# Weights of the dense experts in parts of 80 and 48 first keys instead of two halves of 64, with both weighted one-hots in one instruction and the pair sums in fewer cells

## What is computed

```
def peer_ffn(h, w_q, sub_keys, u_tab, v_tab):
    q = (xc @ w_q).reshape(t, PEER_HEADS, 2, PEER_QDIM // 2)
    sc = jnp.einsum('thpc,hpnc->thpn', q, sub_keys)
    v_half, i_half = lax.top_k(sc, PEER_TOPK_HALF)
    cand = (v_half[:, :, 0, :, None] + v_half[:, :, 1, None, :]).reshape(t, PEER_HEADS, -1)
    cand_idx = (i_half[:, :, 0, :, None] * PEER_NKEYS + i_half[:, :, 1, None, :]).reshape(t, PEER_HEADS, -1)
    top_s, pos = lax.top_k(cand, PEER_TOPK)
    expert = jnp.take_along_axis(cand_idx, pos, axis=-1)
    g = jax.nn.softmax(top_s, axis=-1)
    act = jax.nn.gelu(jnp.einsum('thkd,td->thk', u_tab[expert], xc), approximate=False)
    return jnp.einsum('thk,thkd->td', g * act, v_tab[expert])
```

## Time and profile before

| | |
|---|---|
| median of the runs | 2077.0 us |
| the profiled execution | 2068.39 us, span 2066.6 us |
| TensorE busy | 2007.3 us (97%) |
| VectorE busy | 1622.2 us (78%) |
| ScalarE busy | 857.9 us (42%) |
| GpSimd busy | 385.0 us (19%) |
| moved by DMA | 511.17 MB, mean 247 GB/s |
| granted TensorE clock, mean | 0.992 of full speed |

### The profile page before, as it was taken

One profiled execution on the slowest core, in us unless ns is written; L12 is line 12 of the kernel. 1 busy time (PEld: TensorE's weight loads), 2 busy tenths in 40 slices (PEclk: granted clock), 3 DMA queues, 4 the chain that ended last, 5 costly groups with the idle time before them and its releaser, 6 DMA issues.

```text
span 2066.6 us, 35237 instructions
## 1 busy us (share of the span) xinstructions
PE 2007.3 (97%) x12408; PEld 1791.5 (87%) x12408; DVE 1622.2 (78%) x3208; ACT 857.9 (42%) x1653; POOL 385.0 (19%) x262
## 2 busy tenths in 40 slices
PE   8999999999999999999999999999999999999998
PEld 6888887779999999977887887899999998778786
DVE  6899886865799276699999967639964756999997
ACT  6557454545101100055565666531101002555665
POOL 0000000000024233303243100000352322232440
PEclk9999999999999999999999999999999999999999
DMA  6554344415389989867799853335998988678995
GB/s 258 198 203 163 114 139 156 138 67 174 133 337 341 368 321 327 300 241 229 262 351 356 294 184 117 113 117 195 391 353 309 346 306 317 224 243 281 371 377 181
DMA packets 132634, 511.17 MB, mean 247 GB/s; under 512 B 15004, under 2 KB 15132, under 8 KB 129856
## 3 DMA queue, kind: packets, MB, share of 16 engines
q1 hardware_dynamic: 95680, 375.81, 51.7%
q0 software_dynamic: 36864, 134.23, 17.6%
HBM read 508.94 MB, written 1.05 MB: 247 GB/s over the span
## 4 chain that ended last, share of the span: by engine, by line
PE 64%; DVE 16%; DMA 5%; issue 2%; ACT 2%; SPq 0%; DVEq 0%; ACTq 0%
PE bank L2383 30%; PE bank L344 8%; PE bank L346 8%; PE bank L345 8%; DVE tile_lo L2705 5%; DMA wbuf<-in_peer_v 3%; PE bank L2413 3%; PE bank L2414 3%; DVE x_tok L2258 2%; DMA wbuf<-in_peer_u 2%; PE bank L2282 1%; DVE w_parts L2708 1%; DVE e_hot_first L2274 1%; DVE e_hidden L2290 1%; DVE tile_lo L274 1%
## 5 line engine op out<-in xcount | busy, mean ns | idle before, releaser
L2383 PE MATMUL bank<-h_dense,wbuf 128*128 128x192 f32 x4096 | 679.7, 327 | 3.7 <-ACT e_stage L2467 2.4
L2383 PEld LDWEIGHTS bank<-h_dense,wbuf 128*128 128x128 f32 x4096 | 664.2, 190 | 6.0 <-issue 4.9
L2512 ACT ACTIVATE tile_hi<-wbuf 128x1024 fp32r<-128x1024 f32 x248 | 263.0, 1060 | 246.1 <-DMA wbuf<-in_peer_v 202.3
L2705 DVE TENSOR_TENSOR tile_lo<-wbuf,tile_hi 128x1024 fp32r<-128x1024 f32 x256 | 311.0, 1215 | 37.7 <-ACT tile_hi L2512 27.4
L2244 POOL DMA_INDIRECT e_gbuf<-in_peer_v,e_row_at x128 | 227.1, 1774 | 484.3 <-DVE x_tok L2258 445.8
L2494 ACT ACTIVATE e_hidden<-bank 128x384 f32<-128x384 f32 x128 | 62.7, 490 | 603.2 <-PE bank L2383 603.2
L2244 POOL DMA_INDIRECT e_gbuf<-in_peer_rows,e_row_at x128 | 155.8, 1218 | 470.1 <-DVE e_dots L2252 239.0
L2413 PE MATMUL bank<-tile_hi,w_parts 128*128 128x512 f32 x512 | 208.5, 407 | 11.1 <-DVE w_parts L2708 10.4
L274 DVE TENSOR_TENSOR tile_lo<-wbuf,tile_hi 128x1024 fp32r<-128x1024 f32 (+2 forms) x117 | 140.3, 1212 | 80.1 <-ACT tile_hi L266 79.2
L2414 PE MATMUL bank<-tile_lo,w_parts 128*128 128x512 f32 x512 | 200.4, 391 | 0.0
L344 PE MATMUL bank<-tile_hi,w_parts 128*128 128x512 f32 x512 | 200.1, 391 | 0.0
(11 more groups left out here) (391 smaller groups left out, 3500.3 us busy)
## 6 DMA issues: line engine op xcount, KB each, us to landing
wbuf<-in_peer_u SPq DMA_DIRECT2D x256, 512.0 KB, 5.7
wbuf<-in_peer_v SPq DMA_DIRECT2D x256, 512.0 KB, 5.0
wbuf<-in_w_in SPq DMA_DIRECT2D x16, 2048.0 KB, 7.7
wbuf<-in_peer_q SPq DMA_DIRECT2D x32, 512.0 KB, 3.8
wbuf<-in_hyb_in SPq DMA_DIRECT2D x16, 512.0 KB, 3.7
wbuf<-in_mla_uq SPq DMA_DIRECT2D x9, 512.0 KB, 3.4
wbuf<-in_mla_in SPq DMA_DIRECT2D x8, 528.0 KB, 4.2
wbuf<-in_w_v SPq DMA_DIRECT2D x2, 2048.0 KB, 7.3
```

Source lines behind the costliest of these rows:

```text
L2383: last = nc.tensor.matmul(bank[:, j // 2 % 2, j % 2 * S:j % 2 * S + DENSE], ring[:, slot, k * P:(k + 1) * P], h_dense[:, k, :], start=(k = ...
L2512: nc.scalar.activation(tile_hi[:, slot, 0:D], ring[:, slot, 0:D], ACT.Copy).then_inc(hi_done, 1)
L2705: nc.vector.tensor_tensor(tile_lo[:, slot, 0:D], ring[:, slot, 0:D], tile_hi[:, slot, 0:D].bitcast(F32), ALU.subtract).then_inc(lo_done, 1)
```

## The change

- `PARTS`: the first part is first keys 0 to 79 with groups of 6 tokens (32 groups, 12 matmuls of 80 columns each), the second is keys 80 to 127 with groups of 8 (24 groups, 16 matmuls of 48 columns). `HALF`, `GROUP` and `NGROUP` go.
- The picks are turned after key 79 of U, and the 32 groups of the first part come after keys 80 to 118: after four of every five keys. Keys 120 to 127 have none. The 24 groups of the second part come after every third key from 0 to 69 of V.
- The share's two parts lie together in `pick_parts`, and one multiplication makes both weighted one-hots, twice as many elements as each of the two had. A matmul reads every fourth element of them, before every second.
- `TAKEN` and `LAST_TAKE`: VectorE takes rows 36 to 85 during weighted U (before 36 to 77), rows 86 to 91 during the weighted keys of V (before 78 to 87), the rest by key 118 (before 116).
- The gelu of the dots and the product with the shares come in two pieces (48 and 16), after keys 93 and 103.
- The pair sums of a head are 17 rows of 8 (the first score of one half with all 16 of the other, then each further one with the first 8), 136 cells in place of 256; the place of a pick is turned back into its two indices by a few more small steps.
- `dense_turned` turns 128 x 128 for both halves of the tokens, where the first was 64 x 64; the second writes over what is too much.

```diff
-    HALF = NKEYS // 2
-    GROUP = 8
+    PARTS = ((0, 80, 6), (80, 48, 8))
+    FIRST_KEYS = PARTS[0][1]
     WEIGHT_ONE = 4096.0
-    NGROUP = DENSE // GROUP
+    NGROUPS = [DENSE // group for start, keys, group in PARTS]
...
+    pick_parts = picks_T[:, 2:4, :].rearrange("p w t -> p (w t)").rearrange("p (i w m) -> p i w m", w=2, m=2)
...
-    is_first = [sb(f"{tag}_is_first{b}", [P, PAIRS, HALF, 2], F16) for b in range(2)]
-    hot_first = [sb(f"{tag}_hot_first{b}", [P, 2, PAIRS, HALF, 2], F16) for b in range(2)]
-    hot_second = [sb(f"{tag}_hot_second{b}", [P, PAIRS, NKEYS, 2], F16) for b in range(2)]
+    is_first = [sb(f"{tag}_is_first{b}", [P, most_first], F16) for b in range(2)]
+    hot_first = [sb(f"{tag}_hot_first{b}", [P, 2 * most_first], F16) for b in range(2)]
+    hot_second = [sb(f"{tag}_hot_second{b}", [P, most_second], F16) for b in range(2)]
...
+        weighted_first = hot_first[b][:, 0:2 * group * keys].rearrange("p (i a w m) -> p i a w m", a=keys, w=2, m=2)
...
-        b = n % 2
-        tokens = bass.ds(GROUP * n, GROUP)
-        def pairs(j, keys):
...
-        nc.vector.tensor_tensor(is_first[b][:, :, :, :], wide[:, half * HALF:(half + 1) * HALF, :].unsqueeze(1).to_broadcast([P, PAIRS, HALF, 2]),
-                                pairs(0, HALF), ALU.is_equal).then_inc(first_done, 1)
-        nc.vector.tensor_tensor(hot_second[b][:, :, :, :], wide[:, :, :].unsqueeze(1).to_broadcast([P, PAIRS, NKEYS, 2]),
-                                pairs(1, NKEYS), ALU.is_equal).then_inc(hots_done, 1)
-        dve.wait_ge(first_done, NGROUP * half + n + 1)
...
-        for part in range(2):
-            made = nc.vector.tensor_tensor(hot_first[b][:, part, :, :, :], is_first[b][:, :, :, :], pairs(2 + part, HALF), ALU.mult)
-        made.then_inc(hots_done, 1)
+        start, keys, group = PARTS[half]
+        pairs = group // 2
+        first, weighted_first, second = hots(half, n % 2)
...
+        nc.vector.tensor_tensor(first, wide[:, start:start + keys, :].unsqueeze(1).to_broadcast([P, pairs, keys, 2]),
+                                by_pairs(0, keys), ALU.is_equal).then_inc(first_done, 1)
+        nc.vector.tensor_tensor(second, wide[:, :, :].unsqueeze(1).to_broadcast([P, pairs, NKEYS, 2]),
+                                by_pairs(1, NKEYS), ALU.is_equal).then_inc(hots_done, 1)
+        dve.wait_ge(first_done, NGROUPS[0] * half + n + 1)
+        nc.vector.tensor_tensor(weighted_first, first.unsqueeze(3).to_broadcast([P, pairs, keys, 2, 2]),
+                                pick_parts[:, pairs * n:pairs * n + pairs, :, :].unsqueeze(2).to_broadcast([P, pairs, keys, 2, 2]),
+                                ALU.mult).then_inc(hots_done, 1)
 
     def weights(pe, half, n, b):
-        pe.wait_ge(hots_done, 2 * (NGROUP * half + n + 1))
-        pe.wait_ge(weighted, NGROUP * half + n + 1)
-        for m in range(GROUP):
+        start, keys, group = PARTS[half]
...
+        for m in range(group):
             for part in range(2):
-                last = nc.tensor.matmul(bank[:, 2 + b, m * HALF:(m + 1) * HALF], hot_second[b][:, m // 2, :, m % 2],
-                                        hot_first[b][:, part, m // 2, :, m % 2],
+                last = nc.tensor.matmul(bank[:, 2 + b, m * keys:(m + 1) * keys], second[:, m // 2, :, m % 2],
+                                        weighted_first[:, m // 2, :, part, m % 2],
                                         start=(part == 0), stop=(part == 1))
...
-        nc.vector.scalar_tensor_tensor(out=part, in0=bank[:, 2 + n % 2, 0:GROUP * HALF].rearrange("p (m a) -> p a m", m=GROUP),
+        start, keys, group = PARTS[half]
+        dve.wait_ge(weights_done, NGROUPS[0] * half + n + 1)
+        part = hidden[:, start:start + keys, group * n:group * n + group]
+        nc.vector.scalar_tensor_tensor(out=part, in0=bank[:, 2 + n % 2, 0:group * keys].rearrange("p (m a) -> p a m", m=group),
...
-    FOURS, SIXES, WEIGHING = 3, 2, 7
-    FIRST_WEIGHING = ROUNDS - WEIGHING
-    FOUR_AT = {0: 0, 2: 1, 4: 2, 6: 3}
-    SIX_AT = {0: 0, 2: 1, 5: 2, 7: 3, 10: 4, 12: 5}
-    TAKEN, LAST_TAKE = (16, 30, 36, 78, 88), 116
-    EXPS_AT, ACTS_AT = (16, 30), 54
+    FIRST_WEIGHING, FIRST_LOOPS, FIRST_LOOP = FIRST_KEYS // STEP, 2, 20
+    FIRST_AT = {j: n for n, j in enumerate(j for j in range(FIRST_LOOP) if j % 5 < 4)}
+    SECOND_LOOPS, SECOND_LOOP = 3, 24
+    SECOND_AT = {3 * n: n for n in range(8)}
+    WEIGHING = SECOND_LOOPS * SECOND_LOOP // STEP
+    TAKEN, LAST_TAKE = (16, 30, 36, 86, 92), 118
+    EXPS_AT, ACTS_AT, ACTS = (16, 30), (46, 51), (slice(0, 48), slice(48, SHARED))
+    ROWS_1 = PK + 1
...
         def dense_turned(out, source):
-            nc.tensor.transpose(out[:, 0:LATE], source(slice(0, LATE), 1), ident[0:LATE, 0:LATE])
-            return nc.tensor.transpose(out[:, LATE:DENSE], source(slice(0, P), 0), ident)
+            nc.tensor.transpose(out[:, 0:P], source(1), ident)
+            return nc.tensor.transpose(out[:, LATE:DENSE], source(0), ident)
...
-        with pe.Fori(0, FOURS) as q:
-            for j in range(STEP):
-                experts(q, STEP, FIRST_WEIGHING * STEP, j)
-                if j in FOUR_AT:
-                    weights(pe, 0, 4 * q + FOUR_AT[j], FOUR_AT[j] % 2)
-        with pe.Fori(0, SIXES) as q:
-            for j in range(2 * STEP):
-                experts(q, 2 * STEP, (FIRST_WEIGHING + FOURS) * STEP, j)
-                if j in SIX_AT:
-                    weights(pe, 0, 6 * q + 4 * FOURS + SIX_AT[j], SIX_AT[j] % 2)
+            dense_turned(bank[:, 2 + j // 2, j % 2 * S:j % 2 * S + DENSE], lambda t: pick[:, t, j, :]).then_inc(picks_turned, 1)
+        with pe.Fori(0, FIRST_LOOPS) as q:
+            for j in range(FIRST_LOOP):
+                experts(q, FIRST_LOOP, FIRST_KEYS, j)
+                if j in FIRST_AT:
+                    weights(pe, 0, len(FIRST_AT) * q + FIRST_AT[j], FIRST_AT[j] % 2)
+        for j in range(NKEYS - FIRST_KEYS - FIRST_LOOPS * FIRST_LOOP):
+            experts(0, STEP, FIRST_KEYS + FIRST_LOOPS * FIRST_LOOP, j)
...
-        with pe.Fori(0, FOURS) as q:
-            for j in range(STEP):
-                values(q, STEP, 0, j)
-                if j in FOUR_AT:
-                    weights(pe, 1, 4 * q + FOUR_AT[j], FOUR_AT[j] % 2)
-        with pe.Fori(0, SIXES) as q:
-            for j in range(2 * STEP):
-                values(q, 2 * STEP, FOURS * STEP, j)
-                if j in SIX_AT:
-                    weights(pe, 1, 6 * q + 4 * FOURS + SIX_AT[j], SIX_AT[j] % 2)
+        with pe.Fori(0, SECOND_LOOPS) as q:
+            for j in range(SECOND_LOOP):
+                values(q, SECOND_LOOP, 0, j)
+                if j in SECOND_AT:
+                    weights(pe, 1, len(SECOND_AT) * q + SECOND_AT[j], SECOND_AT[j] % 2)
...
-            if f == ACTS_AT:
-                act.wait_ge(gather_used, GATHER_0 + SHARED)
-                nc.scalar.activation(acts[:, :], dots[:, :], ACT.Gelu).then_inc(exps_done, 1)
...
+            if f in ACTS_AT:
+                part = ACTS[ACTS_AT.index(f)]
+                act.wait_ge(gather_used, GATHER_0 + part.stop)
+                nc.scalar.activation(acts[:, part], dots[:, part], ACT.Gelu).then_inc(exps_done, 1)
...
-            work = half_scores[:, t, :, :].rearrange("p j n -> p (j n)").rearrange("p (h a b) -> p h a b", h=PH, a=PK)
+            cells = half_scores[:, t, :, :].rearrange("p j n -> p (j n)")
+            rows = cells[:, 0:PH * ROWS_1 * 8].rearrange("p (h a b) -> p h a b", h=PH, a=ROWS_1)
+            sums_of = rows.rearrange("p h a b -> p h (a b)")
             by_half = half_best[t].rearrange("p (h c) k -> p h c k", c=2)
-            after(nc.vector.tensor_tensor(work, by_half[:, :, 0, :].unsqueeze(3).to_broadcast([P, PH, PK, PK]),
-                                          by_half[:, :, 1, :].unsqueeze(2).to_broadcast([P, PH, PK, PK]), ALU.add))
+            after(nc.vector.tensor_tensor(sums_of[:, :, 0:PK], by_half[:, :, 0, 0:1].to_broadcast([P, PH, PK]), by_half[:, :, 1, :], ALU.add))
+            after(nc.vector.tensor_tensor(rows[:, :, 2:ROWS_1, :], by_half[:, :, 0, 1:PK].unsqueeze(3).to_broadcast([P, PH, PK - 1, 8]),
+                                          by_half[:, :, 1, 0:8].unsqueeze(2).to_broadcast([P, PH, PK - 1, 8]), ALU.add))
...
-            for c, (op, operand) in enumerate(((ALU.logical_shift_right, 4), (ALU.bitwise_and, PK - 1))):
-                after(nc.vector.tensor_scalar(nibble, place[t], operand, None, op))
-                after(nc.vector.tensor_copy(chosen, nibble))
...
+            after(nc.vector.tensor_scalar(nibble, place[t], 3, None, ALU.logical_shift_right))
+            after(nc.vector.tensor_scalar(chosen, nibble, -1.0, 0.0, ALU.add, ALU.max))
+            keys_of(0)
+            after(nc.vector.tensor_scalar(below_row, nibble, 1.0, 8.0, ALU.is_equal, ALU.mult))
+            after(nc.vector.tensor_scalar(nibble, place[t], 7, None, ALU.bitwise_and))
+            after(nc.vector.tensor_copy(chosen, nibble))
```

(9 more changed lines are left out.)

61 lines of the change are left out of this document (37 added, 24 removed).

## The result

The changed kernel takes **2108.5 us** (median of four runs, 2105.58 to 2114.97) against 2077.85 us (2076.82 to 2086.66) before: a ratio of **1.0142**, 95% interval 1.0105 to 1.018. It is slower by some 30 us, where no change was forecast and the range ended at 2096. The profiled execution took 2110.44 us, its span 2108.6.

The account below looks back on a forecast made before the run. TensorE, busy nearly without a break over the expert tables, was taken as the bound, VectorE counting only where TensorE waits. Seven terms summed to +1.9 us on a profiled 2068.4; carrying 8.6 to the median gave 2079, range 2068 to 2096.

Parts of the forecast that it names:

- parts 1 and 2: Matmul groups in U and V, priced mainly by columns: +6.0 and -3.0 us, together +3.0 us.
- The last rival: TensorE reads the moving operand, now every fourth half-word, more slowly; column time doubled gives +41 us, 2120; chance 0.05.
- Groups in U: Weighted U: 24 groups of 16 64-column matmuls become 32 of 12 with 80 columns; +6.0 us (0 to +6.4).
- Groups in V: Weighted V: 24 groups go from 64 to 48 columns, between column and matmul pricing; -3.0 us (-5.8 to 0).
- Transposes: First transposes, 22 of them, go from 64 by 64 to 128 by 128; +1.3 us (0 to +1.3).
- VectorE in U: Weighted U: VectorE loses its cover and TensorE waits about 1 us a layer; +2.0 us (0 to +6).
- the rival of one element a cycle: Combined weighted one-hots on VectorE run at the single rate: +31 us, 2110; chance 0.06.
- the rival of late rows: Weighted U: gathered rows come late because memory must bring 364 GB/s; 2095 at 340 GB/s; chance 0.17.
- End of U to V: TensorE's stop before V shrinks as V tiles come earlier, with less clock lost; -4.0 us (-6.5 to 0).
- Early V: VectorE gets slack, so TensorE's stops vanish, with about 0.3 us for each restart; -4.9 us (-5.0 to 0).
- Late V: Memory at 345 and 354 GB/s gives stalls of 8.0 and 5.1 us; +4.5 us (-7.7 to +22).
- the first rival: Late V runs without a stall, needing 371 GB/s: -7.7 in place of +4.5 us, taken as 2070; chance 0.25.

Follow-up runs that it names:

- e1: The changed kernel with the two weighted one-hots one behind the other, so matmuls read in steps of 4 bytes: 0.9932 of the kernel before, 0.9909 when repeated.
- e0: The kernel before, unchanged, run again for a second profile: ratio 0.9993, profile span 2066.3 us.
- e6: e1 with the rows of before (40 instead of 36 late in V) and the second gelu piece one pair of keys later: 0.9977 of the kernel before.
- e10: e6, but the 40 rows taken late in V add only 512 of their 1024 columns, with the same memory traffic: 0.9903 of the kernel before.

## Why the prediction was wrong

**The step that failed: parts 1 and 2 took the column time of reads in steps of 4 bytes for reads in steps of 8.** They came to +3.0 us and measured about +44. The last rival held what happened, and its chance was too low. It named the mechanism (each matmul reads every fourth half-word), the condition (the column time doubles) and the price, +41 us. Measured are 0.91 and 0.94 ns a column where it was 0.47, 41.6 us by the rows, 43 by the ratios. It got 0.05. No row of the profile before showed a step other than 4 bytes, so the terms 1 and 2, "by columns", rested on the step staying the same; and the chance leaned on the Trainium skill, "SBUF — State Buffer", Specifications (TRN2), whose two hits on a 16-byte line I read as free at 8 bytes. The runs contradict it for TensorE's moving operand in half precision: two elements in 16 bytes give half the rate, four give all of it. A condition met "at the edge", with +41 us behind it against a sum of +1.9, deserved much more of the chance, and the range should have reached it. The bounds of terms 1 and 2 (0 to +6.4, -5.8 to 0) left it out although no row excluded it.

Had that rival been the forecast, 2120 would still have been 11.5 too high, because the rest of the sum was off as well. Point by point, both layers together, for the step of 4 bytes from e1 against e0 and for the change itself where it differs:

1. *Groups in U*, +6.0: 32 of 0.445 us, 14.2 against 11.6 a layer, +5.3, and with the 0.07 us by which the key behind a group is longer in both kernels **+6.4**. Right at 4 bytes; in the change about +33.
2. *Groups in V*, -3.0: 10.0 against 11.6 a layer, **-3.2**. Right at 4 bytes; in the change +11.5. The figure of the Trainium skill, "TensorE: Matmul & The Clock Gate", Back-to-back issue gap (25 ns for a short matmul, by which I estimate 0.40 us for 16), is close to the 0.42. By the formula that the Trainium skill gives there, parts 1 and 2 come to +1.9 (an estimate), not to the +1.6 of the prediction.
3. *Transposes*, +1.3: **-5.3**, 22 pairs of 0.46 us that became 0.22. I took the difference of two records for the cost, though the starts in the earlier trace rows already lie 0.26 us apart, and never looked at what two equal transposes in a row take. The sign was wrong.
4. *VectorE in U*, +2.0: **0**. The group was scaled rightly (1.93 us: 0.32, 0.47, 0.57, 0.57), and VectorE was full (110.38 of 112 us in e1), but TensorE waited only 0.12 us a layer, before the first group; with 2.2 us more of work a layer it waited 0.85. VectorE's steps from start to start are those four numbers to 0.01 us, 0.57 us for the 960 elements of the combined one-hots, so the rival of one element a cycle is out. Memory gave 382 GB/s there and VectorE waited for no row, so the rival of late rows had no ground either.
5. *End of U to V*, -4.0: idle **-3.8** in e1 (3.83 to 1.98, 2.90 to 0.99), -2.9 in the change against the profile that the forecast started from. In layer 0 the stop of 2.01 us still cost the change some clock (0.66 over the first 5 us of V, where it was 0.50), while e1 kept 1.00 after 1.98 us. Right.
6. *Early V*, -4.9: less than 0.2 us of idle before the groups is left, in every version with the shorter groups and the later picks. V of both layers is 11.7 us shorter in e1 than in e0, the groups are 3.2 of it and late V nothing (below), so **-8.5** is left here, some 2 of it the clock after the stop of layer 0. Right in the mechanism, and too small. No row shows the 0.3 us for each restart that the term used.
7. *Late V*, +4.5: **0**, in the change and in e1. The keys behind the last group run over 2.27 us each by 2.7 and 2.1 us in all in the change, 2.4 and 1.7 in e1. In the kernel before it was 6.3 and 2.2 in the profile that the forecast started from, but 3.2 and 0.9 in e0, and 1.9 and 2.9 with the square transposes alone. So the stalls did not grow to 8.0 and 5.1, and there the first rival was right. They did not vanish either, and most of the 7.7 us that it priced was a matter of one execution. My byte count asked for 371 GB/s with an average of 345 to 354; memory gave 365 to 369 with whole rows, 378 and 385 late in V where VectorE was relieved, and over 400 for 15 us in U. By what e6 and e10 show of VectorE, I took for memory's limit the rate of a stretch in which VectorE and memory take turns as the bound.

So for the change without the step the sum is 6.4 - 3.2 - 5.3 + 0 - 3.8 - 8.5 + 0 = -14.4, where the profiles of e1 and e0 lie 13.7 us apart and the ratios of e1 say -14 to -19. With the step, +41.6 - 14.4 = +27 of the measured 30. Without the step the prediction is off by some 16 us: the transposes (6.6), late V (4.5), early V (3.6) and VectorE in U (2.0), all too slow. The 8.6 us carried from the profile to the median was no property of the kernel: its median was 2068 to 2084 from comparison to comparison.

## What to carry to other kernels

When an edit packs two operands of TensorE into each other to save an instruction elsewhere, look first at the step in bytes with which the matmuls then read: here it cost some 42 us to save 2 to 4, and putting the same two pieces one behind the other kept the saving. A resource that no row shows in its new form has no bound from rows of its old form; its worst case belongs inside the range. And a stage where two engines take turns waiting shows neither one's limit, so shorten one of them before calling the other the bound. Stalls of one profiled execution are no property of the kernel before a second profile repeats them: here 8.5 us of them were 4.0 in the next.

## What the runs showed of the hardware

- A column of a matmul whose moving operand is in half precision takes 0.44 to 0.48 ns with steps of 2 and 4 bytes (80 columns), 0.68 with 6, 0.87 to 0.94 with 8, and 1.9 with 16 and 32.
- A transpose of 64 x 64 beside one of 128 x 128 makes the pair cost 0.46 us; two of 128 x 128 cost 0.22.
- VectorE writes both weighted one-hots in one instruction at the same pace in either layout: 0.65 us for 960 elements.
- Table tiles and gathered rows together reached 378 and 385 GB/s over 106 us and 408 over 15 us, where late V in the earlier trace rows showed 356 to 365.
- A stop of TensorE of about 2 us before V left the granted clock at 1.00 in one kernel (1.98 us, e1) and brought it to 0.66 over the next 5 us in another (2.01 us, the change).
